# Neighbourhood attention tiled by groups of eight columns instead of by grid rows, in a two-block transformer kernel

## What is computed

```
row_start = clip(r - 4, 0, 16 - 8)                 # 8 rows of keys
col_idx   = clip(c - 8, 0, 64 - 16) + arange(16)   # 16 columns of keys
s_loc = einsum('bhcd,bhrckd->bhcrk', q_r, k_win) * scale + bias(rpb, row offset, column offset)
s_ctx = einsum('bhcd,bhjd->bhcj', q_r, kch) * scale            # 256 context keys
p = softmax(concatenate([s_loc, s_ctx]))
o = p_loc @ v_win + p_ctx @ v_ctx ;  y = o * silu(g)
```

## Time and profile before

| | before |
|---|---|
| device time, median of 3 runs | 3994.05 us (3992.76 to 3996.78) |
| span of the profiled execution, its own time | 3989.9 us |
| TensorE busy | 89% |
| VectorE busy | 39% |
| ScalarE busy | 33% |
| TensorE, mean granted clock | 0.932 |
| six units of neighbourhood attention | 785.3 us together |

### The profile page before, as it was taken

How to read it: one execution, slowest core, us unless ns; L and a number is a source line. 1 busy time by engine, 2 the same in 40 slices (tenths; PEclk the granted TensorE clock), 3 DMA queues, 4 the chain that set the end, 5 groups by cost and what they waited for, 6 DMA issues and landing times.

```text
span 3989.9 us, 45425 instructions
## 1 busy us (share of the span) xinstructions
PE 3558.6 (89%) x18676; PEld 2754.5 (69%) x18676; DVE 1573.4 (39%) x3007; ACT 1315.7 (33%) x2213; POOL 70.2 (2%) x113
## 2 busy tenths in 40 slices
PE   9988888988979889988968889789888899999997
PEld 8866667767847667666737677666656678777885
DVE  3333343344354334444334455533333433323322
ACT  3122233333262223433353323322322433323322
POOL 1000000000000000000000000000000000000000
PEclk9988899898989889999989999899977999999998
DMA  5111101103331000102320000000001222223222
GB/s 199 64 39 40 54 22 44 44 22 113 103 109 43 27 32 22 32 22 74 108 81 28 17 17 17 27 22 27 27 16 48 79 91 95 76 88 111 95 90 69
DMA packets 61709, 232.57 MB, mean 58 GB/s; under 512 B 7162, under 2 KB 7288, under 8 KB 60736
## 3 DMA queue, kind: packets, MB, share of 16 engines
q1 hardware_dynamic: 47520, 170.94, 13.2%
q0 software_dynamic: 13984, 58.73, 4.2%
HBM read 208.80 MB, written 20.84 MB: 58 GB/s over the span
## 4 chain that ended last, share of the span: by engine, by line
PE 48%; DVE 7%; ACT 5%; issue 2%; DMA 0%; ACTq 0%; DVEq 0%; POOL 0%
PE bank L275 33%; PE bank L2153 2%; PE bank L2132 2%; PE bank L1839 1%; ACT ws L239 1%; PE bank L1189 1%; PE bank L1848 1%; PE bank L2141 1%; PE bank L1222 1%; PE bank L439 1%; DVE ws L247 1%; PE bank L1847 1%; DVE ar L1897 1%; PE bank L503 1%; PE bank L1192 0%
## 5 line engine op out<-in xcount | busy, mean ns | idle before, releaser
L275 PE MATMUL bank<-HH,ws 128*128 128x512 f32 (+1 forms) x5088 | 1143.9, 381 | 35.1 <-DVE HH L1552 18.9
L275 PEld LDWEIGHTS bank<-HH,ws 128*128 128x128 f32 x5088 | 892.1, 196 | 212.6 <-issue 39.2
L247 DVE TENSOR_TENSOR ws<-raw,ws 128x1024 fp32r<-128x1024 f32 (+1 forms) x282 | 341.1, 1210 | 940.9 <-ACT ws L239 940.3
L275 PE MATMUL bank<-HF,ws 128*128 128x512 f32 x2112 | 497.6, 398 | 11.5 <-DVE ws L247 11.5
L275 PE MATMUL bank<-H,ws 128*128 128x512 f32 x1776 | 476.2, 423 | 23.9 <-DVE ws L247 15.0
L275 PEld LDWEIGHTS bank<-HF,ws 128*128 128x128 f32 x2112 | 401.0, 190 | 107.9 <-DVE ws L247 12.4
L275 PEld LDWEIGHTS bank<-H,ws 128*128 128x128 f32 x1776 | 349.8, 201 | 117.9 <-DVE ws L247 17.1
L239 ACT ACTIVATE ws<-raw 128x1024 fp32r<-128x1024 f32 (+1 forms) x282 | 293.3, 1041 | 133.7 <-PE bank L275 130.3
L275 PE MATMUL bank<-FF,ws 128*128 128x512 f32 x1056 | 255.3, 402 | 4.4 <-DVE ws L247 4.4
L275 PEld LDWEIGHTS bank<-FF,ws 128*128 128x128 f32 x1056 | 200.3, 190 | 57.0 <-issue 5.8
L775 ACT ACTIVATE Y<-bank 128x256 f32<-128x256 f32 (+1 forms) x152 | 82.6, 544 | 381.1 <-PE bank L275 381.1
(11 more groups left out here) (375 smaller groups left out, 3945.2 us busy)
## 6 DMA issues: line engine op xcount, KB each, us to landing
raw<-in_win SPq DMA_DIRECT2D x96, 512.0 KB, 3.6
raw<-in_wmod SPq DMA_DIRECT2D x48, 512.0 KB, 4.6
raw<-in_wout SPq DMA_DIRECT2D x48, 512.0 KB, 3.6
raw<-in_wgate SPq DMA_DIRECT2D x44, 512.0 KB, 3.6
raw<-in_wup SPq DMA_DIRECT2D x44, 512.0 KB, 3.6
raw<-in_wdown SPq DMA_DIRECT2D x32, 512.0 KB, 3.5
x<-Y POOLq DMA_DIRECT2D x4, 2048.0 KB, 8.3
raw<-in_wdown SPq DMA_DIRECT2D x16, 384.0 KB, 3.1
```

The lines of the kernel that those rows point to most:

```text
L247: dve.tensor_tensor(ws[:, b % SPLIT, 1, 0:n], raw[:, blk["r"] % RAW, 0:n], ws[:, b % SPLIT, 0, 0:n].bitcast(F32), ALU.subtract).then_inc(s ...
L275: mm = pe.matmul(bank[o % 2][:, 0:n], ws[:, b % SPLIT, wp, k * P:(k + 1) * P], blk["rhs"](xp, blk["k0"] + k, t0, n), start=blk["first"] an ...
```

## The change

The queries go by **groups of 8 columns** (`CW`) over all 16 rows: 128 queries of one head. Their local keys are the group and its neighbours on either side: 384 keys, and 256 for the first and the last group. K, V and Q are stored in that order by the evacuation of their projections (`by_columns`). A head's scores are a multiplication of its own 64 channels, head 0 on partitions 0 to 63, head 1 on 64 to 127, into banks of their own, without `QB`. There are 8 steps of the grid (and 2 of the context in the first layer), each with both heads. The bias, with the windows of rows and columns in it, is a table of 12 blocks of 128 by 128 for each pair of heads. It is gathered when the inputs are laid out, and a unit's table (768 KB) is loaded while the unit before it runs. `rpb_phase`, the reversal, the mask, `VS` and `QB` go. `PT` has two buffers, and `values(i - 1)` comes after the turns of step i. There are two points of `fill()` in a step.

```diff
-N1 = _place(C1, [..., ("pairmask", P), ("flip64", P), ..., ("wincol", GRID_W), ...
+N1 = _place(C1, [..., ("pairmask", P), ...
+CW = P // GRID_H
+GROUPS = GRID_W // CW
...
-        QB = spot(20 * P, 0)
-        NT = spot(RPB_H * GRID_W)
-        PR = [spot(768), spot(768)]
+        NB = [spot(12 * P, TMP_N), spot(12 * P)]
         VT = spot(T)
-        VS, LL, PT = spot(7 * P), spot(1024), spot(768)
+        PR = [spot(10 * P).rearrange("q (e x) -> q e x", e=2) for _ in range(2)]
+        PT = [spot(10 * P) for _ in range(2)]
...
@@ ret_unit (the last of a layer)
+            def pool(g):
+                g.wait_ge(*s_rope.at(n_rope))
+                load_bias_na(g, l, 0)
...
-        def rpb_phase():
...
+        def load_bias_na(g, l, p):
+            g.dma_start(NB[p % 2], I["nb"][PAIRS * l + p]).then_inc(s_nb[p % 2].sem, 16)
...
@@ na_unit
+            def by_columns(dst, scale=1.0):
+                def evac(act, ci, t0, n, ps):
+                    if t0 < CTX:
+                        return act.activation(dst[:, t0:t0 + n], ps, ACT.Copy, scale=scale)
+                    r0, k = (t0 - CTX) // GRID_W, n // GRID_W
+                    to = dst[:, CTX:].rearrange("q (g r i) -> q g r i", r=GRID_H, i=CW)[:, :, r0:r0 + k, :].rearrange("q g r i -> q r g i")
+                    return act.activation(to, ps.rearrange("q (r g i) -> q r g i", r=k, i=CW), ACT.Copy, scale=scale)
+                return evac
...
-            fills = [("t", range(0, 4)), ("t", range(4, 8)), ("t", range(8, 10)), ("s", range(0, 4)), ("s", range(4, 7))]
+            fills = [range(0, 4), range(4, 8), range(8, 10)]
+            local = [(max(g - 1, 0), min(g + 1, GROUPS - 1)) if kind == "grid" else (0, -1) for kind, g in steps]
+            split = [[(e, 0, nb) for e in range(2)] if nb == 2 else [(e, a, b) for e in range(2) for a, b in ((0, nb - 2), (nb - 2, nb))] for nb in nblk]
...
@@ TensorE
+                def scores(i):
+                    a, b = local[i]
+                    if nloc[i]:
+                        for e in range(2):
+                            r = slice(64 * e, 64 * e + 64)
+                            if i and nloc[i - 1]:
+                                pt.wait_ge(*s_m.at(2 * i - 1 + e))
+                            if e == 0 and i >= 3:
+                                pt.wait_ge(*s_y.at(i - 2))
+                            pt.matmul(bank[2 + e][:, 0:nloc[i]], Qb[r, q0[i]:q0[i] + P], Kb[r, CTX + P * a:CTX + P * (b + 1)],
+                                      start=True, stop=True).then_inc(s_s.sem, 1)
+                    if i:
+                        pt.wait_ge(*s_e.at(2 * i))
+                    for e in range(2):
+                        r = slice(64 * e, 64 * e + 64)
+                        pt.matmul(bank[4 + e][:, 0:CTX], Qb[r, q0[i]:q0[i] + P], Kb[r, 0:CTX],
+                                  start=True, stop=True).then_inc(s_s.sem, 1)
+                def turn(i, j):
+                    e, b0, b1 = split[i][j]
+                    gi = gfirst[i] + j
+                    pt.wait_ge(*s_pn.at(2 * i + e + 1))
+                    if gi >= 2:
+                        pt.wait_ge(*(s_ca, s_cd)[gi % 2].at(gi // 2))
+                    for b in range(b0, b1):
+                        mm = pt.transpose(bank[6 + gi % 2][:, (b - b0) * P:(b - b0 + 1) * P], PR[i % 2][:, e, b * P:(b + 1) * P], k1("ident"))
+                    mm.then_inc(s_t.sem, 1)
+                def values(i):
...
+                    for b in range(n):
+                        v = local[i][0] + 2 + b if b < n - 2 else b - (n - 2)
+                        for e in range(2):
+                            mm = pt.matmul(bank[2][64 * e:64 * e + 64, 0:P], VT[:, v * P + 64 * e:v * P + 64 * e + 64],
+                                           PT[i % 2][:, (e * n + b) * P:(e * n + b + 1) * P], start=b == 0, stop=b == n - 1)
...
                 for i in range(R):
                     if i + 1 < R:
                         scores(i + 1)
-                    turn(i)
-                    fill()
-                    values(i)
+                    half = len(split[i]) // 2
+                    for j in range(half):
+                        turn(i, j)
+                    fill()
+                    for j in range(half, 2 * half):
+                        turn(i, j)
+                    if i:
+                        values(i - 1)
+                    fill()
+                values(R - 1)
@@ ScalarE
                 for i in range(R):
+                    copy(i, 0)
                     if i + 1 < R:
                         exps(i + 1)
-                    evac_pt(i)
+                    fill()
+                    if len(split[i]) == 4:
+                        copy(i, 2)
                     fill()
@@ VectorE
                 for i in range(R):
                     norm(i)
+                    if i + 1 < R:
+                        maxes(i + 1, 0)
+                    copy(i, 1)
+                    if i + 1 < R:
+                        maxes(i + 1, 1)
+                    fill()
+                    if len(split[i]) == 4:
+                        copy(i, 3)
+                    if i:
+                        result(i - 1)
                     fill()
...
-            unit = dict(u=u, blks=allb, points=len(fills) + R, ...
+            unit = dict(u=u, blks=allb, points=len(fills) + 2 * R, ...
...
-                   ..., rpb_phase(), bias_rows,
+                   ..., bias_rows,
```

More of the change, by code:

```diff
@@ new lines, in na_unit @@
+            R = len(steps)
+            local = [(max(g - 1, 0), min(g + 1, GROUPS - 1)) if kind == "grid" else (0, -1) for kind, g in steps]
+            nloc = [P * (b - a + 1) for a, b in local]
+            nblk = [n // P + CTX // P for n in nloc]
+            q0 = [P * g + (CTX if kind == "grid" else 0) for kind, g in steps]
+            n_scores = [0]
+            for kind, g in steps:
+                n_scores.append(n_scores[-1] + (4 if kind == "grid" else 2))
+            split = [[(e, 0, nb) for e in range(2)] if nb == 2 else [(e, a, b) for e in range(2) for a, b in ((0, nb - 2), (nb - 2, nb))] for nb in nblk]
@@ L1171, in pe @@
+                scores(0)
+                for f, ns in enumerate(fills):
                     if f >= 2:
@@ new lines, in act, with exps, copy @@
+            def act(a, fill):
+                def exps(i):
+                    if i >= 2 and nloc[i] == 0:
+                        a.wait_ge(*s_t.at(gfirst[i - 1]))
+                    for e in range(2):
+                        a.wait_ge(*s_m.at(2 * i + e + 1))
+                        n = nloc[i]
+                        if n:
+                            a.activation(PR[i % 2][:, e, 0:n], PR[i % 2][:, e, 0:n], ACT.Exp, bias=field(i, 2, e), accum_out=field(i, 3, e))
+                        a.activation(PR[i % 2][:, e, n:n + CTX], bank[4 + e][:, 0:CTX], ACT.Exp, bias=field(i, 2, e),
+                                     accum_out=field(i, 4, e)).then_inc(s_e.sem, 1)
+                def copy(i, j):
+                    e, b0, b1 = split[i][j]
+                    if j == 0 and i >= 2:
+                        a.wait_ge(*s_o.at(i - 1))
+                    a.wait_ge(*s_t.at(gfirst[i] + j + 1))
+                    at = (e * nblk[i] + b0) * P
+                    a.activation(PT[i % 2][:, at:at + (b1 - b0) * P], bank[6][:, 0:(b1 - b0) * P], ACT.Copy).then_inc(s_ca.sem, 1)
+                exps(0)
+                for f, ns in enumerate(fills):
@@ new lines, in copy, with result @@
+                def copy(i, j):
+                    e, b0, b1 = split[i][j]
+                    if j == 1 and i >= 2:
+                        v.wait_ge(*s_o.at(i - 1))
+                    v.wait_ge(*s_t.at(gfirst[i] + j + 1))
+                    at = (e * nblk[i] + b0) * P
+                    v.tensor_copy(PT[i % 2][:, at:at + (b1 - b0) * P], bank[7][:, 0:(b1 - b0) * P]).then_inc(s_cd.sem, 1)
+                def result(i):
+                    v.wait_ge(*s_o.at(i + 1))
+                    if i == 0:
+                        v.wait_ge(*got[3][-1])
+                    kind, g = steps[i]
+                    o = bank[2][:, 0:P]
+                    if kind == "ctx":
+                        y = Gb[:, g * P:(g + 1) * P]
+                    else:
+                        y = Gb[:, CTX:].rearrange("q (r g i) -> q r g i", g=GROUPS, i=CW)[:, :, g, :]
+                        o = o.rearrange("q (r i) -> q r i", i=CW)
+                    v.tensor_tensor(y, o, y, ALU.mult).then_inc(s_y.sem, 1)
@@ L1343, in dve @@
                 v.wait_ge(*s_unit.at(u + 1))
[L1345 removed]
+            unit = dict(u=u, blks=allb, points=len(fills) + 2 * R, act_first=act_first(l, u), result=Gb, pe=pe, act=act, dve=dve, pool=pool)
             store(unit, 5 + p, lo)
```

272 lines of the change are left out of this document (84 added, 188 removed).

## The result

| | before | after |
|---|---|---|
| device time, median | 3994.95 us (4 runs) | 3770.32 us (3769.38 to 3772.61, 4 runs) |
| ratio to before, 95% interval | | 0.944 (0.942 to 0.945) |
| span of the profiled execution | 3989.9 us | 3768.5 us |
| six units of neighbourhood attention | 785.3 us | 566.8 us |
| TensorE idle in them | 81.9 us | 16.5 us |

The kernel is 5.6% faster. It forecast 155 us saved; 225 were.

A forecast was written before the change was run, and what follows sets the result against it. The prediction took TensorE's work and the idle time between its pieces as the bound: 3989.9 - 108 (work) - 42 (gaps) - 5 (clock) = 3835 us, plus 4.2 for the runs' median, 3839 us; range 3795 to 3912.

The forecast's parts named there:

- a chain over VectorE: Rival in the grid's steps: VectorE's fill waits for ScalarE's rounding, some 1.5 us late a step, 3911 us; chance 0.19.
- The gaps: TensorE's idle time in the six units: 40 of 81.9 us stay, 42 us won (10 to 60).
- a cycle of 5.1: Shortest cycle of a grid step, from head 0's context turn: 5.1 us at most against 8.6 of TensorE's work.
- The end of a unit: Gap expected at the end of every unit, where values and result come one after the other: 1.5 us.
- VectorE in a fill behind ScalarE's split: Gap expected in the units where VectorE stands in a fill behind ScalarE's split; no size of its own.
- The wait at the start of the first unit of a layer: Gap expected where TensorE waits for the unit before; no size of its own.
- The clock: Low clock in the six units, about 40 us together: fewer long gaps win 5 us (0 to 20).
- The work on TensorE: Multiplications and turns in the six units: 108 us less (24 at the dear end, 123 at the cheap one).
- the cheap end of 123: TensorE's work saved in six units if its small pieces come at their low prices: 123 us.
- Heads that don't overlap: Rival on TensorE: row and column halves run one after the other, 3923 us; chance 0.17, in part or whole.
- The handover of bank 2: Rival: scores wait for the result in the values' bank; a loss from 3.2 us a step, 4031 at 4; chance 0.03.
- What was costed at nothing: Off the path: evacuation in column order 0.6 us for 512 columns, as now, hidden; bias table lands in about 6 us.

The follow-up runs named there:

- experiment 2: The changed kernel with the late values undone, each step's values multiplied in their own step, tiling by columns kept: 3806.59 us.
- Experiment 7: The kernel before with ten turns of no use ahead of the wait for each row's values: 4035.11 us.
- the kernels in step: The changed kernel with values in their own step, and the same with the result ahead of the normalization: 3806.59 and 3809.42 us.
- experiments 4 and 5: The changed kernel with values of one head after the other, 3799.42 us; the changed kernel with scores of one head after the other, 3773.85 us.
- experiment 6: The changed kernel with the first of a step's two fills moved behind the values, next to the second: 3790.65 us.
- experiment 1: The kernel before, tiling by rows kept, with a second buffer for the turned weights and values one row later: 3946.6 us.

## Why the prediction was wrong

The mechanism was right in the main: TensorE's work bounds the units, both kinds of halves overlap, the waits for the copies are gone, and a chain over VectorE shows in one unit of six only. One part of it was not as told: with the new tiling the waits for the copies go even without the late values, which are worth their 36 us through bank 2 (experiment 2). Three terms of the sum were too small, and all erred the same way.

- **The gaps.** The step that failed most for its size: "Some gaps stay ... I put them at 40 of the 81.9 us, so **42 us** are won (... 60 at best)". 16.5 us stay, and 65.4 were won. The prediction's own working had 8.6 us of TensorE's work against a cycle of 5.1, which leaves nothing waiting in a normal step, and then 40 us for the exceptions: 6.7 us a unit, with no row behind it. Its three reasons measured small. The end of a unit: the second layer's middle unit has 0.46 us of idle time in all (82.20 - 81.74), its end included. VectorE in a fill behind ScalarE's split: real, but only in the last unit, 3.9 us. The wait at the start of the first unit of a layer: real (4.3 us), but ahead of that unit's window, before and after.
- **The clock.** "The fewer long gaps, the less: **5 us** (0 to 20)" measured up to 26.3. By that price most of the low clock would have stayed whatever the gaps did, for which no row was given. Experiment 7 shows the contrary: gaps filled, and 35 of the 43 us are gone. In the kernels in step the clock still costs 26 to 28 us at 45 to 50 us of idle time.
- **The work on TensorE.** 108 us predicted, 127 measured, above the cheap end of 123. 12 us of it is the price of a step: scores 1.28 for 1.6 and turns 1.16 for 1.1 with values 1.24 for 1.25 make 3.68 for 3.95, and a unit's grid 28.0 us for 30.0. The scores were put between overlap and none, "nearer to the overlap"; it was complete. The other 7 us is what the old rows cost beyond 2.82 us each, about 1 us a unit: in the unit from 1610.10 the five kinds of pieces of sixteen rows add up to some 46 us at full clock, not 45.1. That one row, picked where it had no gap, stood for sixteen.
- **The range.** Its low end took cheap values of all three terms together, 198 us (which makes 3796 us, written as 3795), and each of them came out beyond it: 65 for 55, up to 26 for 20, 127 for 123. Gaps and clock go together here (experiment 7), so a low end with few gaps needed a larger gain at the clock.
- **The rivals.** Heads that don't overlap: shown wrong by experiments 4 and 5; that the values would lose 29 us if the order did not alternate shows what the overlap carries. A chain over VectorE, its fill behind ScalarE's rounding: it shows three times, 3.9 us, and not in most steps; with both fills in one place (experiment 6) a wait for a copy does come back in every step, 0.5 us each. The handover of bank 2: it costs 3.0 us in the first layer's units, in waits of at most 0.5 us, and 2.8 in the second's, 1.8 of them the wait at 1594.16. With the values in their own step it is the largest wait: 19.9 us there in experiment 2.
- **Order and tiling.** From the four kernels, rows or columns, in step or late (3995, 3947, 3807, 3770): the late order is worth 48 us on rows and 36 on columns, the tiling 188 in step and 176 late. The tiling's part holds 33 us of gaps (81.9 to 49.0).
- What was costed at nothing cost nothing. The evacuation into runs of 8 elements takes 594 ns for 512 columns (line 1125), against 593 for the plain one it stands in for; the bias table never shows as a wait.

## What to carry to other kernels

A consumer that is one step late, on a second buffer, and the new tiling with its longer step each closed about 40% of the gaps here when made alone (31.5 and 32.9 of 81.9 us), and 80% together, and the order alone was worth 37 us more in a phase that nobody had touched; look for `values(i)` at the end of its own step. When a sum says that nothing waits in a normal step, believe it, and price the exceptions from rows. Price idle time of TensorE above its length, since the low clock that follows goes with it, and move both ends of the range together. Many multiplications on halves of the array belong in alternation, block by block; for the four of the scores the order made no difference.

## What the hardware showed that was not expected

A gap of about 2 us can be enough for a low clock. TensorE's timeline in a second-layer unit before, and a window of 3 us in it:

```profile
1629.24 1.06 PE L1192 MATMUL bank<-Y,arena 128*128 128x256 f32 x2 [2.01 <-ACT arena L1261]
1630.29 1.11 PE L1202 MATMUL bank<-c,arena 128*128 128x128 f32 x4
```

```profile
1629.50:1632.50 3.00, 3.00 (x11) 2.11 (x11) 2.46 (x7) 0.72 (x2) 0.00 (x0) 0.50 0.00 0
```

The ten microseconds from 1617.0 have no idle time and a clock of 1.00; behind the wait the clock is at the lower level, and six turns cost 1.19 us (1630.29 to 1631.48) for 0.58 in the earlier trace rows. Of the 15 waits of 2.0 to 2.6 us inside the six units before, 13 have such a fall at them; in experiment 1 most waits of the same length have none. So it is no rule that these traces give.

Nor is a gap needed. In the kernel after, one case with a gap, in front of the products for the modulation (line 260, each over 2 columns), and one without:

```profile
489.47 2.84 PE L260 MATMUL bank<-cact,raw 128*128 128x2 f32 x16 [2.21 <-ACT Y L1125]
517.66 1.95 PE L260 MATMUL bank<-cact,raw 128*128 128x2 f32 x16
```

```profile
490.00:500.00 10.00, 10.00 (x59) 8.68 (x60) 2.67 (x10) 2.20 (x9) 0.00 (x0) 0.66 0.30 105
511.40:520.90 9.50, 9.50 (x72) 7.40 (x72) 4.93 (x16) 3.75 (x11) 0.00 (x0) 1.00 0.03 6
521.00:524.00 3.00, 3.00 (x16) 3.00 (x16) 2.33 (x9) 1.75 (x6) 0.00 (x0) 0.50 0.81 325
```

From 511.40 on TensorE is never idle, and at 521.0 its clock is low all the same, 1.5 us behind sixteen of these small products; the same happens at 626.8, but not behind those at 781.5. No run varies these products by themselves, so what brings such a fall is open, and part of the 16.7 us that the clock still costs after need not be the gaps' doing. In experiment 6 the same products run with no gap ahead of them and no fall follows, and there the many waits of 0.5 us bring none either: its units in the first layer have a clock of 0.97, 1.00 and 1.00, and the one fall inside the units comes with a wait of 2.5 us. TensorE's turns, where they filled gaps, kept the clock up (experiment 7).

The look-ahead over halves of the array is the other surprise: the scores by head lose nothing, and the values by head, with up to ten records in a row on one half, still have about half of the overlap, and in both TensorE passed three waiting records.
